# Transformer stack, one core: the two convolution feed-forwards also read the unscaled residual row

## The reference, cut to what matters

```
def rms_norm(x, g):
    y = xf * rsqrt(mean(xf * xf, -1) + EPS)      # one factor per token
    return y * g                                 # one gain per feature

def conv_ffn(x, w_up, conv_w, conv_b, w_down):   # x = rms_norm(h, g)
    u = x @ w_up                                 # 1024 -> 2 * 2816
    c = conv_b + sum(conv_w[j] * shifted(u, j) for j in range(3))   # along the tokens
    g, val = c[..., :2816], c[..., 2816:]
    return (gelu(g) * val) @ w_down
h = h + rms_norm(mixer, g1);  h = h + rms_norm(conv_ffn(rms_norm(h, g2)), g3)
```

## Time and profile before

| what | value |
|---|---|
| median of three runs | 1143.19 us (1141.84 to 1143.56) |
| the profiled execution | 1138.24 us, its span 1136.4 us |
| granted TensorE clock, mean | 0.997 |
| ACT busy | 692.6 us (61%) |
| chain that ended last, by engine | PE 92%, DVE 3%, ACT 2% |
| high part of down weights, L1606 | 1046 ns each, 88 times |
| low part of down weights, L2150 | 1217 ns each, 88 times |
| middle tap, L1724; cross products out, L1716 | 601 ns, 377 ns |
| side tap, L2328; sum of one half, L2300 | 482 ns, 421 ns |
| low part of 1024 columns of weights, L2117 | 970 ns as a mean over 7 forms |

### The profile page before, as it was taken

One profiled execution on the slowest core, in us unless ns is written; L12 is line 12 of the kernel. 1 busy time (PEld: TensorE's weight loads), 2 busy tenths in 40 slices (PEclk: granted clock), 3 DMA queues, 4 the chain that ended last, 5 costly groups with the idle time before them and its releaser, 6 DMA issues.

```text
span 1136.4 us, 19022 instructions
## 1 busy us (share of the span) xinstructions
PE 1118.5 (98%) x6585; PEld 969.1 (85%) x6585; DVE 823.1 (72%) x1272; ACT 692.6 (61%) x1216; POOL 48.4 (4%) x71
## 2 busy tenths in 40 slices
PE   9999999999999999999999999999999999999997
PEld 7987888888899878888888888888996788888886
DVE  5866888888767578888887766666656757766665
ACT  6666766766655666766666554556585845555553
POOL 0100000000100000000000000000000320000000
PEclk9999999999999999999999999999999999999999
DMA  7705666757434455766654766664684005876761
GB/s 260 246 1 155 189 196 201 215 174 230 144 117 148 164 153 168 215 195 199 201 170 145 221 198 192 189 180 141 188 278 149 2 23 166 222 219 176 199 162 63
DMA packets 237172, 194.74 MB, mean 171 GB/s; under 512 B 11230, under 2 KB 219712, under 8 KB 237120
## 3 DMA queue, kind: packets, MB, share of 16 engines
q1 hardware_dynamic: 237040, 194.01, 56.8%
q10 hardware_dynamic: 80, 0.03, 0.0%
HBM read 192.97 MB, written 1.05 MB: 171 GB/s over the span
## 4 chain that ended last, share of the span: by engine, by line
PE 92%; DVE 3%; ACT 2%; issue 1%; POOL 0%; DMA 0%; POOLq 0%; DVEq 0%; SPq 0%; ACTq 0%
PE psum L921 26%; PE psum L926 14%; PE psum L954 7%; PE psum L957 7%; PE psum L961 7%; PE psum L697 6%; PE psum L699 6%; PE psum L698 6%; ACT arena L2042 1%; DVE resid_eps L2235 1%; PE psum L907 1%; PE psum L1206 1%; PE psum L911 1%; PE psum L908 1%; PE psum L753 1%
## 5 line engine op out<-in xcount | busy, mean ns | idle before, releaser
L921 PE MATMUL psum<-act_hl,hi_u 128*128 128x512 f32 x1312 | 326.8, 391 | 0.0
L2145 DVE TENSOR_TENSOR lo_u<-raw_u,hi_u 128x2048 fp32r<-128x2048 f32 x103 | 236.0, 2292 | 77.5 <-ACT hi_u L1597 39.9
L921 PEld LDWEIGHTS psum<-act_hl,hi_u 128*128 128x128 f32 x1312 | 240.6, 188 | 46.4
L926 PEld LDWEIGHTS psum<-act_hl,lo_u 128*128 128x128 f32 x1312 | 179.0, 190 | 12.8
L926 PE MATMUL psum<-act_hl,lo_u 128*128 128x256 f32 x1312 | 182.9, 282 | 0.0
L1597 ACT ACTIVATE hi_u<-raw_u 128x2048 fp32r<-128x2048 f32 x68 | 129.7, 1908 | 15.2 <-DMA raw_u<-in_ffn_w_gu 15.1
L1716 ACT ACTIVATE arena<-psum 128x256 f32<-128x256 f32 x174 | 64.7, 377 | 99.0 <-PE psum L926 91.3
L2300 DVE TENSOR_TENSOR arena<-psum,arena 128x256 f32<-128x256 f32 x174 | 72.9, 421 | 69.8 <-ACT arena L1716 69.6
L2150 DVE TENSOR_TENSOR lo_d<-raw_d,hi_d 128x1024 fp32r<-128x1024 f32 x88 | 106.8, 1217 | 8.5 <-ACT hi_d L1606 8.5
L2328 DVE SCALAR_TENSOR_TENSOR arena<-arena,vecs 128x255 f32<-128x255 f32 x176 | 84.9, 482 | 37.9 <-ACT arena L1724 26.9
L2117 DVE TENSOR_TENSOR lo_u<-raw_u,hi_u 128x1024 fp32r<-128x1024 f32 (+6 forms) x84 | 78.1, 970 | 27.5 <-ACT hi_u L1576 27.3
(11 more groups left out here) (312 smaller groups left out, 1786.9 us busy)
## 6 DMA issues: line engine op xcount, KB each, us to landing
raw_u<-in_ffn_w_up SPq DMA_DIRECT2D x88, 512.0 KB, 5.6
raw_d<-in_ffn_w_down SPq DMA_DIRECT2D x86, 512.0 KB, 3.4
raw_u<-in_ffn_w_gu SPq DMA_DIRECT2D x84, 512.0 KB, 5.7
raw_u<-in_diff_w_qkv SPq DMA_DIRECT2D x24, 512.0 KB, 4.6
raw_u<-in_w_in SPq DMA_DIRECT2D x24, 512.0 KB, 4.6
raw_u<-in_mla_w_o SPq DMA_DIRECT2D x8, 512.0 KB, 4.4
raw_u<-in_diff_w_o SPq DMA_DIRECT2D x8, 512.0 KB, 4.4
raw_u<-in_w_out SPq DMA_DIRECT2D x8, 512.0 KB, 4.5
```

The lines of the kernel that those rows point to most:

```text
L921: pe.matmul(o, hi[:, k, :], act_hl[:, k].rearrange("p a t -> p (a t)"), start=k == 0, stop=False)
L926: mm = pe.matmul(o[:, SEQ:], lo[:, k, :], act_hl[:, k, 0, :], start=False, stop=k == KC - 1)
L2145: dve.tensor_tensor(v[0], v[1], v[2].bitcast(F32), ALU.subtract).then_inc(S("lo_u_done"), 1)
```

## The change

`UNSCALED` now holds N_F0 and N_F1 too, so that both convolution feed-forwards go the second way. The factors are turned after the fourth product of tile 1's gate half, in all four feed-forwards. For the convolution feed-forwards the two sums become one instruction of 512 columns (`both_summed`), and one of 512 columns that multiplies by the factors is new (`both_scaled`); both wait for both halves of the products. ACT's two middle taps come ahead of the gelu. In tile 0, ACT does a two-column gelu (or silu) behind `split_u(2)`. In tile 21 sum and scaling go by halves. The splitting of the next stage's first unit moves from tile 20 into tile 21 on ACT, and behind the last hidden low part on DVE.

```
-UNSCALED = [N_DIFF, N_F2, N_F3]
+UNSCALED = [N_F0, N_DIFF, N_F1, N_F2, N_F3]
# PE, up(1)
                         for k in range(KC):
                             pe.matmul(o, hi[:, k, :], ...)
+                            if isinstance(t, int) and t == 1 and s == 0 and k == 3 and i in UNSCALED:
+                                factors_turn(i)
...
-                        if isinstance(t, int) and t == 1 and s == 0 and i in UNSCALED:
-                            factors_turn(i)
# PE, ACT and DVE, at N_F0 and N_F1
-            norm_transposes(N_F0)
+            resid_transposes(N_F0)
-            norm(N_F0)
+            resid_norm(N_F0)
# ACT, tile
                     if b is None and t < 2:
...
-                        if f < 2:
+                        if t == 1 and f < 2:
                             conv_mid(0, cg)
+                            conv_mid(1, cv)
                         split_u(u + 2)
-                    elif f < 2:
+                        if t == 0:
+                            gate = ACT.Gelu_apprx_tanh if f < 2 else ACT.Silu
+                            act.wait_ge(S("half_set"), 1)
+                            act.activation(st[:, ST_OF["hgrn"], 8 + 2 * f:10 + 2 * f], half[:, 0:2], gate)
+                        if t == 0 and f < 2:
+                            conv_mid(0, cg)
+                            conv_mid(1, cv)
+                    elif f < 2 and t == FT - 1:
+                        split_d(g)
                         conv_mid(0, cg)
                         cross_out(1)
+                        split_part(u + 1, 0)
+                        conv_mid(1, cv)
+                    elif f < 2:
+                        cross_out(1)
+                        conv_mid(0, cg)
+                        conv_mid(1, cv)
                     if f < 2:
                         act.wait_ge(S("tap_b"), at2(2 * g + 1))
                         act.activation(gg..., cg..., ACT.Gelu_apprx_tanh)
-                        conv_mid(1, cv)
...
-                    elif 2 <= t < 21:
+                    elif 2 <= t < 21 - (f < 2):
                         split_u(u + 2)
+                    elif f < 2 and t == FT - 1:
+                        split_part(u + 1, 1)
...
-                    if t == 20:
+                    if t == 20 and f >= 2:
                         split_d(g + 1)
# DVE, tile
+                    def both_summed():
+                        dve.wait_ge(S("cross_out"), at2(2 * g + 2))
+                        dve.tensor_tensor(cross[:, slot], psum[:, 4 + 2 * slot:6 + 2 * slot, 0:SEQ], cross[:, slot], ALU.add)
+                    def both_scaled():
+                        dve.wait_ge(S("gate_raw"), at(raw_sums + 1))
+                        dve.tensor_tensor(up_sum[:, slot], cross[:, slot], row_factors (both halves), ALU.mult)
...
+                    if f < 2 and t == FT - 1:
+                        hidden_low(g - 1, 1 - slot, P)
+                        split_d(g - 1)
+                        half_summed(0)
+                        half_scaled(0)
+                        split_d(g)
+                        half_summed(1)
+                        half_scaled(1)
+                    elif f < 2:
+                        both_summed()
+                        if b is not None or t:
+                            both_scaled()
...
+                    if b is None and t == 0:
+                        factors_out()
+                        if f < 2:
+                            both_scaled()
+                        else:
+                            gate_scaled()
+                        split_u(u + 2)
                     if f < 2:
                         taps(0, cg)
+                        if t == FT - 1:
+                            taps(1, cv)
+                    if b is None and t == 1:
                         split_u(u + 2)
...
-                    if t == 20 and f < 2:
-                        split_half(u + 2, 0)
-                    elif b is not None or 2 <= t < 21:
+                    if b is not None or 2 <= t < 21 - (f < 2):
                         split_u(u + 2, b)
-                    if t == 20:
+                    if t == 20 and f >= 2:
                         split_d(g)
                         split_d(g + 1)
                     if t == 21:
                         hidden_low(g, slot, n)
                         if f < 2:
+                            split_half(u + 1, 0)
                             split_half(u + 1, 1)
```

More of the change, by code:

```diff
@@ L1548, in _ @@
             diff()
-            norm_transposes(N_F1)
+            resid_transposes(N_F1)
             ffn(1)
@@ L2093, in _ @@
             diff()
-            norm(N_F1)
+            resid_norm(N_F1)
             ffn(1)
@@ L2305, in sum_up, with half_summed, half_scaled @@
                             summed.then_inc(S("up_sum"), 1)
+                    def both_summed():
+                        dve.wait_ge(S("cross_out"), at2(2 * g + 2))
+                        dve.tensor_tensor(cross[:, slot], psum[:, 4 + 2 * slot:6 + 2 * slot, 0:SEQ], cross[:, slot], ALU.add)\
+                            .then_inc(S("gate_raw"), 1)
+                    def both_scaled():
+                        dve.wait_ge(S("gate_raw"), at(raw_sums + 1))
+                        dve.tensor_tensor(up_sum[:, slot], cross[:, slot], row_factors.unsqueeze(1).broadcast_to([P, 2, SEQ]),
+                                          ALU.mult).then_inc(S("up_sum"), 2)
+                    def half_summed(part):
+                        dve.wait_ge(S("cross_out"), 2 * g + part + 1)
+                        dve.tensor_tensor(cross[:, slot, part], psum[:, 4 + 2 * slot + part, 0:SEQ], cross[:, slot, part],
+                                          ALU.add).then_inc(S("gate_raw"), 1)
+                    def half_scaled(part):
+                        dve.wait_ge(S("gate_raw"), raw_sums + part + 1)
+                        dve.tensor_tensor(up_sum[:, slot, part], cross[:, slot, part], row_factors, ALU.mult)\
+                            .then_inc(S("up_sum"), 1)
                     def gate_scaled():
-                        dve.wait_ge(S("gate_raw"), at(g - 2 * FT + 1))
+                        dve.wait_ge(S("gate_raw"), at(raw_sums + 1))
                         dve.tensor_tensor(cg[0:n, slot, :], up_sum[0:n, slot, 0, :], row_factors[0:n, :], ALU.mult)\
@@ L2336, in hidden_low @@
                                           ALU.subtract).then_inc(S("hid_lo_done"), 1)
-                    sum_up(0)
-                    if f >= 2 and (b is not None or t):
-                        gate_scaled()
+                    if f < 2 and t == FT - 1:
[11 more added lines that the diff above has]
+                    else:
+                        sum_up(0)
+                        if b is not None or t:
+                            gate_scaled()
                     if b is not None or 0 < t < 21:
@@ L2344, in tile @@
                         hidden_low(g - 1, 1 - slot, P)
[L2345 removed]
+                    if b is None and t < 2 and f >= 2:
                         sum_up(1)
[L2347 to L2348 removed]
+                    if b is None and t == 0:
+                        factors_out()
+                        if f < 2:
+                            both_scaled()
+                        else:
+                            gate_scaled()
+                        split_u(u + 2)
                     if f < 2:
                         taps(0, cg)
[L2351 removed]
+                        if t == FT - 1:
+                            taps(1, cv)
+                    if b is None and t == 1:
                         split_u(u + 2)
[L2353 to L2356 removed]
+                    elif n == P and f >= 2 and (b is not None or t):
                         sum_up(1)
@@ L2361, in tile @@
                     if f < 2:
-                        taps(1, cv)
+                        if t != FT - 1:
+                            taps(1, cv)
                         dve.wait_ge(S("tap_b"), at2(2 * g + 2))
```

14 lines of the change are left out of this document (4 added, 10 removed).

## The result

The changed kernel takes 1150.13 us (median of 8 runs, 1145.85 to 1151.11) where the kernel before takes 1142.19 (median of 8 runs beside it). The ratio is 1.0065, with a 95% interval of 1.0051 to 1.008: 7.4 us slower, between 5.8 and 9.1 (the medians are 7.9 apart). The forecast was +3.1 us, less than half of it. The direction is right.

The account below looks back on a forecast made before the run. PE was taken to bound the kernel, DVE having least room. Per convolution feed-forward -2.74 + 0.21 + 0.24 + 1.4 + 1.85 + 0.68 = +1.64; twice, less 0.16, +3.1 us: 1146.3, range 1141.0 to 1150.5.

Parts of the forecast that it names:

- Entry, -2.74: Start of each convolution feed-forward: from the row's last updates to the first product 1.80 us instead of 4.54, gaining 2.74.
- transposes +0.21, turn +0.24: PE in tiles 0 and 1: transposes of two chunks lengthen tile 0 by 0.21 us, turning the factors lengthens tile 1 by 0.24.
- First tiles, +1.4: Start of each convolution feed-forward: PE waits at unit 4 for its high part (0.9 us), then its low part (0.5).
- no stall at the start: Rival, 28%: the first tiles' chain is shorter, PE doesn't wait for unit 4; +0.3 us in all, 1143.5.
- The loop, 0: Middle tiles: DVE's round becomes 8.08 us against PE's 8.31, so DVE keeps up and PE loses nothing.
- the lag shrinks to nothing over 16 tiles: Loop: DVE's lag of about 3.7 us behind the first stall is worked off by its 0.23 us of room per round.
- The last tiles, +1.85: Tile 21 of each convolution feed-forward: its hidden tile comes late, so PE idles 1.85 us before the last down product.
- The faster case (tile 21 meets PE): Rival, 13%: tile 21's first tokens come in time, no stall or post norm delay; 1138.4 with no starting stall either.
- DVE bound in the loop: Rival, 17%: wide instructions of 0.84 us make DVE's round 8.40, over PE's 8.31, and lag reaches the last tile; 1156.
- Behind them, +0.68: After the last tiles: extra splitting on DVE delays the post norm, and PE's wait for the row, by 0.68 us.
- Third and fourth feed-forward, -0.16: Tile 2 there: the gate is scaled earlier, so a wait of 0.08 us goes in each.
- The rule weighed: Tile 0's table load: the skill's 1380 ns drain after it would make 1148.7 us; the forecast kept 1.28 us without drain.

Follow-up runs that it names:

- The entry alone: Kernel before, convolution feed-forwards reading the unscaled row with factors turned but never scaling by them, first and last tiles as before: 1137.51 us, ratio 0.9956.
- Products in the gap: Changed kernel with 12 throwaway TensorE products in the idle stretch ahead of the last tile's first down product, convolution feed-forwards only: 1146.77 us, ratio 1.004.
- the three moves: Changed kernel; tile 2's halves both crossed within tile 1, last but one tile's down weights split before its hidden values, value taps before the GELU wait: 1141.16 us.
- the repeat: Changed kernel run again unaltered, as reference for the follow-up runs: 1148.58 us, ratio 1.006 against the kernel before.
- the value taps first: Changed kernel with VectorE's two value taps put ahead of its wait for ScalarE's GELU, tiles 0 to 20 of the convolution feed-forwards: 1147.31 us, ratio 1.0046.
- both halves crossed: Changed kernel with both halves of tile 2 crossed out of PSUM by ScalarE within tile 1, not only the first: 1144.38 us, ratio 1.002.
- the other order of the last down products: Changed kernel with both token halves of tile 20, then both of tile 21, instead of alternating, in the convolution feed-forwards: 1145.99 us, ratio 1.0039.
- the up split ahead: Changed kernel with ScalarE's up-weight split before the middle taps: 1193.50 us alone; 1186.31 with value taps before the GELU wait; 1182.42 with all four moves.

## Why the forecast was right in sign and short in size

Step by step, for the first feed-forward; the second agrees within 0.1 us.

- **Entry, -2.74, transposes +0.21, turn +0.24.** Held: 1.79 us from update to product, tile 2 earlier by 2.23, or by 2.29 as forecast when counted from the update, which starts 0.06 later here. The entry alone gave 5.0 us for both feed-forwards, 4.6 forecast.
- **First tiles, +1.4.** Held: up(4) waits for the high part and then for the low part, 1.05 and 0.53, together 1.58, behind the cross copy that the forecast named (17.1 after tile 1's start by the forecast, 125.65 - 108.58 = 17.07 in the trace). The case "no stall at the start" fell.
- **The loop, 0.** For PE itself it held. The sub-step "the lag shrinks to nothing over 16 tiles" failed. The lag began as forecast: tile 4's products end at 138.20, the sum could follow 0.58 later (in the kernel before, tile 20's products end at 271.76 and the copy ends at 272.34), and it starts at 142.35, a lag of 3.57 where 3.7 stood. But it shrinks by 8.306 - 8.141 = 0.165 in a tile, not 0.23: 2.64 in 16 tiles. At tile 20, whose products end at 271.10, the sum is 272.61 - (271.10 + 0.58) = 0.93 us late. An error of 0.06 us in the round was multiplied by 16, and a remainder that had been set to zero stood in the open. The error is the scaling, which starts 0.79 behind the sum and not 0.72: the forecast took the 0.04 us between two dependent instructions from a pair of 256 columns, and here, with 512 columns, it is 0.10. The margin of 0.23 was the thing to carry in both directions.
- **The last tiles, +1.85.** The mechanism and its length held: from tile 20's sum to L944 it is 13.78 us, where the forecast has 286.03 - 272.34 = 13.69. With the lag of 0.93 and 0.1 of chain the idling is 2.87 us (from 283.52, when the product was due, to 286.39) in place of 1.85; the profile's 2.71 for it starts at the modelled end of the product ahead. The faster case (tile 21 meets PE) and "DVE bound in the loop" fell as stated; but the second one's mechanism, a lag that adds itself to the last tile, was a quarter true at a round of 8.14.
- **Not in the forecast: the clock, +1.68.** The forecast priced the idling by its length and put the clock behind it at nothing. The last down products take 5.57 us in place of 3.89 behind the gap. Products in the gap take this away.
- **Behind them, +0.68.** The first post norm piece did start the moment DVE was free, but it cost nothing in this kernel, since PE's slow products were later still: DVE waits 0.93 us for them at 292.64. With the clock held (products in the gap, the three moves) the transposes wait 0.6 us for DVE, and the term is there.

The sum: forecast +1.64 for a feed-forward; 0.18 more at the first tiles, 1.02 more idling at the last, 1.68 for the clock, less 0.68 for the hidden post norm, make +3.84; the trace has 295.93 - 292.07 = +3.86 at the next stage's first product. Twice this is the +7.67 at the third feed-forward and lies, within the interval, at the 7.4 us of the ratio.

- **Third and fourth feed-forward, -0.16.** From the third's first product to the end it is 534.42 in the repeat and 534.82 before, at the same clock in the mixer. This is not against the term, which is too small to show.
- **The rule weighed.** The trace shows no drain: a load of 1.28 us and the next instruction 0.01 us behind it. The Trainium skill, ScalarE: Activation LUTs, section "What ACT_TABLE_LOAD costs", would have had another 1380 ns there; the measurement decides, and the 1.28 us stand. The 1148.7 us that came out by it are nearer to the measured median, for another reason.

## What to carry to other kernels

An engine that keeps pace with 2% to spare can hide an addition in every tile and still not work off the lateness that it brings along (2.64 of 3.57 us here): work out what lag is left when the loop ends, since the last tile pays it in full, and carry the error of the round times the number of rounds. Price a gap of PE not by its length alone but also by the products behind it. And before work is pulled into an engine's idle stretch, look at when its input lands: an idle stretch in front of a late use can be what hides a transfer.

## What the runs showed of the hardware

TensorE's granted clock falls from 2.4 GHz to 1.2 GHz for a while behind some gaps of about 2.5 us and not behind others; in the changed kernel it is 0.50 of full speed from 288 to 290. With PE busy without a gap for over 140 us before, gaps of 2.71, 2.73 (the changed kernel), 2.71, 2.71 (its repeat), 2.49 and 2.51 us (the value taps first) were each followed by products of 0.63 us, the last down products taking 5.54 to 5.58 us in all. Gaps of 2.63 and 2.64 us (both halves crossed) were followed by products of 0.39, 3.96 us in all. Products of 0.39 also followed gaps of 1.52, 1.35, 1.11 and 1.09. But with the other order of the last down products, a wait of 1.93 us, which begins about 3.5 us behind that gap of 1.35, was followed by half clock in one feed-forward, and a wait of 1.95 at the same place in the other was not. Longer gaps, 4.38 and 3.53 us in the runs with the up split ahead (where PE had waits in the loop too), were followed by 0.63 again. So the length of a gap alone doesn't decide in the stretch from 1.9 to 2.7 us; what does, these runs don't settle. Nor does the drop come at a fixed product: with the value taps first the first product after the gap is already slow (L944 at 285.75 took 0.65), while in the second feed-forward of the changed kernel five are still fast and the sixth is the first slow one (L949 at 600.71 took 0.39, L950 at 600.94 took 0.53). In the mixer's stage the clock differs between executions of one and the same kernel (0.90 and 0.97 in 875 to 925), and the part behind the third feed-forward's first product differs by 2.9 us, which is why a milestone ahead of it tells more than the span.
